# A hybrid decoder layer on one core: the first key chunk takes the place of the 112-column product, which moves into the fourth chunk, and x and the weights are loaded alternately

## The reference, cut to what matters

```python
u = rms_norm(h, norm_mix_w)
proj = u @ w_in                      # [256, 2048] @ [2048, 17504], float32
(q, k_c, v_c, k_s, v_s, k_w, v_w, nsa_gate, z, xbc, dt_raw, branch_gate) = split(proj)
o_nsa = nsa_mixer(q, k_c, ..., nsa_gate, cos, sin, compression weights)   # compressed, selected, window
o_ssm = mamba2_mixer(z, xbc, dt_raw, ...)
merged = sigmoid(gate_a) * (o_nsa @ w_proj_nsa) + sigmoid(gate_b) * (o_ssm @ w_proj_ssm)
h = h + merged @ w_out
h = h + square(relu(rms_norm(h, norm_mlp_w) @ w_up)) @ w_down
out = rms_norm(h, norm_final_w)
```

## Time and profile before

| quantity | value |
|---|---|
| runs | 2144.05, 2144.53, 2145.13 us (median 2144.53) |
| profiled execution, own time | 2145.07 us |
| its span, first to last instruction | 2143.3 us |
| TensorE busy | 98% of the span |
| VectorE, ScalarE, GpSimd busy | 61%, 46%, 9% |
| mean DMA rate over the span | 175 GB/s |
| mean granted TensorE clock | 0.997 |

### The profile page before, as it was taken

The page is one execution under the profiler, slowest core; times in us unless marked ns, Lnnn a source line. Parts: engine busy times, 40 slices in busy tenths (PEclk is TensorE's granted clock), DMA queues, the critical chain, the costliest instruction groups (busy, mean ns, idle before and its releaser), DMA issues.

```text
span 2143.3 us, 28254 instructions
## 1 busy us (share of the span) xinstructions
PE 2098.7 (98%) x9822; PEld 1742.4 (81%) x9822; DVE 1315.3 (61%) x1653; ACT 979.7 (46%) x1339; POOL 186.3 (9%) x226
## 2 busy tenths in 40 slices
PE   7999999999999999999999999999999999999997
PEld 5888888888888887778878778888888888888886
DVE  5646666666664677776577756555555555555554
ACT  5434545454543555554355544444434434444443
POOL 3000000000000033331133310000000000000000
PEclk9999999999999999999999999999999999999999
DMA  8556454545456655545645456556566566556653
GB/s 236 188 162 176 146 169 147 169 146 172 145 184 194 177 157 148 146 148 195 187 139 152 152 187 206 184 180 187 189 194 186 186 196 188 186 191 189 188 190 135
DMA packets 195448, 375.15 MB, mean 175 GB/s; under 512 B 16048, under 2 KB 16144, under 8 KB 194960
## 3 DMA queue, kind: packets, MB, share of 16 engines
q1 hardware_dynamic: 193152, 365.87, 55.9%
q0 software_dynamic: 2160, 7.79, 1.1%
q10 hardware_dynamic: 32, 0.01, 0.0%
HBM read 371.52 MB, written 2.10 MB: 174 GB/s over the span
## 4 chain that ended last, share of the span: by engine, by line
PE 52%; issue 41%; POOL 2%; DVE 1%; ACT 1%; DMA 1%; DVEq 1%; ACTq 0%; POOLq 0%; SPq 0%
PE acc L280 15%; PE acc L282 15%; PE acc L281 15%; PE x L813 1%; PE tr L303 1%; DMA raw<-w_in 1%; POOL ML L600 1%; POOL MH L600 1%; PE x L741 1%; PE x L696 1%; PE tr L763 1%; POOL XTOK L607 1%; PE x L803 0%; PE x L748 0%; PE tr L756 0%
## 5 line engine op out<-in xcount | busy, mean ns | idle before, releaser
L247 DVE TENSOR_TENSOR lo<-raw,hi 128x1024 fp32r<-128x1024 f32 (+1 forms) x696 | 861.3, 1246 | 617.1 <-ACT hi L240 606.6
L240 ACT ACTIVATE hi<-raw 128x1024 fp32r<-128x1024 f32 (+1 forms) x696 | 726.7, 1051 | 676.4 <-PE acc L282 650.6
L280 PE MATMUL acc<-hi,LAh 128*128 128x512 f32 x1856 | 737.5, 397 | 5.0 <-DVE lo L247 5.0
L282 PE MATMUL acc<-hi,LAl 128*128 128x512 f32 x1856 | 724.1, 390 | 0.0
L281 PE MATMUL acc<-lo,LAh 128*128 128x512 f32 x1856 | 723.2, 390 | 0.0
L280 PEld LDWEIGHTS acc<-hi,LAh 128*128 128x128 f32 x1856 | 348.6, 188 | 80.1 <-DVE lo L247 5.3
L282 PEld LDWEIGHTS acc<-hi,LAl 128*128 128x128 f32 x1856 | 348.4, 188 | 73.5
L281 PEld LDWEIGHTS acc<-lo,LAh 128*128 128x128 f32 x1856 | 348.7, 188 | 72.2 <-issue 1.7
L280 PE MATMUL acc<-hi,LBh 128*128 128x512 f32 x896 | 352.1, 393 | 3.2 <-DVE LBl L335 3.2
L282 PE MATMUL acc<-hi,LBl 128*128 128x512 f32 x896 | 349.8, 390 | 0.0
L281 PE MATMUL acc<-lo,LBh 128*128 128x512 f32 x896 | 349.7, 390 | 0.0
(11 more groups left out here) (271 smaller groups left out, 1258.5 us busy)
## 6 DMA issues: line engine op xcount, KB each, us to landing
raw<-w_in SPq DMA_DIRECT2D x304, 512.0 KB, 3.8
raw<-w_up SPq DMA_DIRECT2D x128, 512.0 KB, 3.8
raw<-w_down SPq DMA_DIRECT2D x128, 512.0 KB, 4.5
raw<-w_proj_ssm SPq DMA_DIRECT2D x64, 512.0 KB, 4.2
raw<-w_proj_nsa SPq DMA_DIRECT2D x32, 512.0 KB, 4.6
raw<-w_out SPq DMA_DIRECT2D x32, 512.0 KB, 4.5
GA<-x SPq DMA_DIRECT2D x4, 512.0 KB, 6.0
GA<-cmp_k_w POOLq DMA_DIRECT2D x4, 512.0 KB, 8.9
```

What stands on the lines that cost most here:

```text
L240: act.activation(hi[:, sl, :, 0:n], raw[:, sl, :, 0:n], ACT.Copy).then_inc(s_hi, 1)
L247: dve.tensor_tensor(lo[:, sl, :, 0:n], raw[:, sl, :, 0:n], hi[:, sl, :, 0:n].bitcast(F32), ALU.subtract).then_inc(s_lo, 1)
L280: pe.matmul(o, xh, wh, start=(k == 0), stop=False)
L282: x = pe.matmul(o, xl, wh, start=False, stop=(k == KT - 1))
```

## The change

- C_SMALL is dropped from the row of chunks; C_KC is number 0, all later numbers fall by one, and the two accumulator pairs are swapped for them.
- SP issues x quarter 0, groups 0 and 1 of C_KC, quarter 1, group 2, quarter 2, groups 3 and 4, quarter 3, groups 5 to 7. Group 4 waits for `s_lo` 1, and quarter 3 stands behind it.
- TensorE turns quarters 0 and 1, then multiplies group 0 and turns quarter 2 behind it, and turns quarter 3 behind group 3. Groups 0, 2, 4 and 6 wait for the low parts of quarters 0 to 3. ScalarE and VectorE split in the matching order.
- ScalarE does a one-element copy right after the constants are made, so that its first table load comes there.
- The sums of squares move to slots 3 and 4 of C_KC; the take of C_KC waits for the norm factors.
- The 112 columns: POOL loads all their weights (48 and 64 columns of 2048 rows) into GA after `compress(0)`; ScalarE and VectorE split them whole in C_VS into `LBh` and `LBl`; TensorE multiplies them in four parts behind groups 3 to 6 of C_VS into bank x7. The copy, turn, gates, softplus, cumulative sums and the rest of that chain move into C_VS slot 7, C_KW and C_VW.
- `columns`, `angles` and both `reduce_angles` move to slots 1, 3 and 4 of C_VC, `sines` to its slot 5. `compress_k2` no longer waits for the step sizes.
- The quarters of the compression weights wait for `s_lo` 4 to 18 in twos.

```diff
-C_SMALL, C_KC, C_VC, C_KS, C_VS, C_KW, C_VW, C_AT = 0, 1, 2, 3, 4, 5, 6, 7
+C_KC, C_VC, C_KS, C_VS, C_KW, C_VW, C_AT = 0, 1, 2, 3, 4, 5, 6
...
+            load_x(0)
+            load_group(sp, C_KC, 0, w_in, 0, KC0)
+            load_group(sp, C_KC, 1, w_in, 0, KC0)
+            load_x(1)
+            load_group(sp, C_KC, 2, w_in, 0, KC0)
+            load_x(2)
+            load_group(sp, C_KC, 3, w_in, 0, KC0)
+            load_group(sp, C_KC, 4, w_in, 0, KC0)
+            load_x(3)
+            for j in (5, 6, 7):
+                load_group(sp, C_KC, j, w_in, 0, KC0)
...
-                    pool.wait_ge(s_lo, 8 * n + 2 * q + 6)
+                    pool.wait_ge(s_lo, 8 * n + 2 * q + 4)
...
+            pool.wait_ge(s_hid, 1)
+            pool.dma_start(SMG, w_in[:, :, NG0:NG0 + 3 * NH]).then_inc(s_smw, 16)
+            pool.dma_start(SMD, w_in[:, :, DT0:DT0 + SH]).then_inc(s_smw, 16)
...
+            def small(q):
+                pe.wait_ge(s_sml, 2)
+                o = X7[0:SMALL, 0:S]
+                for k in range(4 * q, 4 * q + 4):
+                    wh, wl = LBh[:, k, 0:SMALL], LBl[:, k, 0:SMALL]
                     pe.matmul(o, wh, LAh[:, k, :], start=(k == 0), stop=False)
                     pe.matmul(o, wh, LAl[:, k, :], start=False, stop=False)
                     x = pe.matmul(o, wl, LAh[:, k, :], start=False, stop=(k == KT - 1))
...
             def compress_k2():
                 pe.wait_ge(s_hs, 1)
                 pe.wait_ge(s_w2, 32)
-                pe.wait_ge(s_dts, 3)
+                pe.wait_ge(s_colc, 2)
...
+            turn_x(0)
+            turn_x(1)
+            mm_chunk(pe, C_KC, 0, LAh, LAl, {0: [lambda: turn_x(2)], 3: [lambda: turn_x(3)]},
+                     need={0: [(s_trd, 1)], 2: [(s_trd, 2)], 4: [(s_trd, 3)], 6: [(s_trd, 4)]})
+            mm_chunk(pe, C_VC, 1, LAh, LAl, {0: [turn_columns], 2: [lambda: pe_turn(pe, E_KC, XR, [(s_acc, C_KC + 1)])],
                                              6: [lambda: compress(0)]})
...
+                                             3: [lambda: small(0)], 4: [lambda: small(1)], 5: [lambda: small(2)],
+                                             6: [lambda: small(3)]})
+            mm_chunk(pe, C_KW, 0, LAh, LAl, {0: [turn_small], 6: [cumsum]})
...
+            act.wait_ge(s_const, 1)
+            act.activation(SS2[:, 0, 0:1], mhalf[:, 0:1], ACT.Copy)
...
+            split_x(0)
+            split_hi(act, C_KC, 0)
+            split_x(1)
+            split_hi(act, C_KC, 1)
+            split_hi(act, C_KC, 2)
+            split_x(2)
...
+            slots(act, split_hi, C_KC, 8, {2: [lambda: split_x(3)], 3: [lambda: squares_of_x(0)], 4: [lambda: squares_of_x(1)],
+                                           7: [take_kc]})
+            slots(act, split_hi, C_VC, 8, {2: [lambda: copy_t(E_KC, KV[:, 0:2, :])], 5: [sines], 6: [lambda: hidden(0, 1)],
+                                           7: [lambda: take(C_VC, 1, XR[:, 0, :])]})
...
+            slots(act, split_hi, C_VS, 8, {0: [small_hi], 2: [lambda: copy_t(E_KS, key_cols(0, 0))],
+                                           7: [lambda: take(C_VS, 1, V_(0, 0)), copy_small]})
+            slots(act, split_hi, C_KW, 8, {1: [gates_dt], 2: [softplus], 7: [lambda: take(C_KW, 0, XR[:, 0, :])]})
...
+            slots(dve, split_lo, C_KC, 8, {2: [lambda: split_x(3)], 7: [take_kc]})
+            slots(dve, split_lo, C_VC, 8, {1: [columns], 2: [lambda: blocks(0, E_KC, CPK)], 3: [angles, lambda: reduce_angles(0)],
+                                           4: [lambda: reduce_angles(1)], 6: [lambda: hidden(0)],
+                                           7: [lambda: take(C_VC, 1, XR[:, 1, :], C_VC + 1)]})
...
+            slots(dve, split_lo, C_KW, 8, {1: [gates_dt], 3: [softplus], 6: [cumsums], 7: [lambda: take_rope(C_KW, 0, C_KW + 1)]})
```

More of the change, by code:

```diff
@@ L158, in build @@
         s_w2 = sem("compression_second_weights_landed")
+        s_smw = sem("small_weights_landed")
+        s_smh = sem("small_high_parts")
+        s_sml = sem("small_low_parts")
+        s_smm = sem("small_multiplied")
+        s_sma = sem("first_small_rows_taken")
+        s_smd = sem("second_small_rows_taken")
         s_smt = sem("gates_copied")
@@ L452, in _, with load_x @@
         def _(sp):
-            for n in range(4):
+            def load_x(n):
                 sp.dma_start(GA[:, :, NC * n:NC * (n + 1)], x_rows[:, :, NC * n:NC * (n + 1)]).then_inc(s_x[n], 16)
+            load_x(0)
[9 more added lines that the diff above has]
+                load_group(sp, C_KC, j, w_in, 0, KC0)
             w_na = a["w_proj_nsa"].rearrange("(k p) c -> p k c", p=P)
@@ L459, in _ @@
             w_dn = a["w_down"].rearrange("(k p) c -> p k c", p=P)
-            load_chunk(sp, C_SMALL, w_in, 0, 0, extra=[(w_in, NG0, 0, 3 * NH), (w_in, DT0, 3 * NH, SH)])
-            for C, c0 in ((C_KC, KC0), (C_VC, VC0), (C_KS, KS0), (C_VS, VS0), (C_KW, KW0), (C_VW, VW0)):
+            for C, c0 in ((C_VC, VC0), (C_KS, KS0), (C_VS, VS0), (C_KW, KW0), (C_VW, VW0)):
                 load_chunk(sp, C, w_in, 0, c0)
@@ L650, in _, with turn_x @@
             pe.transpose(X6[:, 0:16], NAT[0:16, 4, :], identf[0:16, 0:16]).then_inc(s_colp, 1)
-            for n in range(4):
+            def turn_x(n):
                 free = [(s_tra, 2 * n - 2), (s_trd, n - 1)] if n > 1 else []
                 pe_turn(pe, E_U + n, GA[:, :, NC * n:NC * (n + 1)], [(s_x[n], 16)] + free, banks=UB[n % 2], sm=s_tr)
[L656 to L662, removed]
+            def small(q):
[3 more added lines that the diff above has]
+                    wh, wl = LBh[:, k, 0:SMALL], LBl[:, k, 0:SMALL]
                     pe.matmul(o, wh, LAh[:, k, :], start=(k == 0), stop=False)
@@ L950, in hidden @@
                 act.activation(HT[:, :], X7[:, 0:NG * NCMP], ACT.Tanh, scale=0.5).then_inc(s_hta, 1)
[L952 to L955, removed]
@@ L956, in _, with take_kc @@
-            slots(act, split_hi, C_KS, 8, {2: [lambda: copy_t(E_VC, KV[:, 0:2, :])], 6: [lambda: hidden(1, 4)],
[L957 to L962, removed]
+            def take_kc():
+                act.wait_ge(s_rx, 1)
+                take(C_KC, 0, XR[:, 0, :])
@@ L1152, in _, with split_x @@
             dve.drain().then_inc(s_colc, 1)
-            for n in range(4):
+            def split_x(n):
                 dve_split_t(dve, E_U + n, LAh, LAl, 4 * n, COLS[:, CN1 + 4 * n:CN1 + 4 * n + 4], banks=UB[n % 2])
-                if n == 1:
-                    for j in range(LEAD):
-                        split_lo(dve, C_SMALL, j)
+            split_x(0)
+            split_lo(dve, C_KC, 0)
+            split_x(1)
+            split_lo(dve, C_KC, 1)
+            split_lo(dve, C_KC, 2)
+            split_x(2)
             def columns():
@@ L1288, in take_rope, with small_lo @@
                 rope()
[L1290 to L1294, removed]
+            def small_lo():
+                for n, (c0, c1, src) in enumerate(((0, 3 * NH, SMG), (3 * NH, SMALL, SMD))):
+                    dve.wait_ge(s_smh, n + 1)
+                    dve.tensor_tensor(LBl[:, :, c0:c1], src, LBh[:, :, c0:c1].bitcast(F32), ALU.subtract).then_inc(s_sml, 1)
@@ L1295, in _ @@
             dve.wait_ge(s_sin, 4)
             slots(dve, split_lo, C_KS, 8, {1: [key_rope], 2: [lambda: blocks(1, E_VC, CPV)], 5: [key_copy],
[L1297 to L1300, removed]
@@ L1301, in _ @@
-            slots(dve, split_lo, C_VW, 8, {2: [lambda: copy_t(E_KW, key_cols(1, 2))],
-                                           7: [lambda: take(C_VW, 0, V_(1, 1), C_VW + 1)]})
+                                           6: [lambda: hidden(1)], 7: [lambda: take_rope(C_KS, 0, C_KS + 1)]})
+            slots(dve, split_lo, C_VS, 8, {1: [value_copy, small_lo], 2: [lambda: copy_t(E_KS, key_cols(0, 2))],
+                                           7: [lambda: take(C_VS, 1, V_(1, 0), C_VS + 1)]})
+            slots(dve, split_lo, C_KW, 8, {1: [gates_dt], 3: [softplus], 6: [cumsums], 7: [lambda: take_rope(C_KW, 0, C_KW + 1)]})
@@ L1304, in maxima @@
+            slots(dve, split_lo, C_VW, 8, {1: [low_steps], 2: [lambda: copy_t(E_KW, key_cols(1, 2))],
+                                           7: [lambda: take(C_VW, 1, V_(1, 1), C_VW + 1)]})
             def maxima(n):
```

76 lines of the change are left out of this document (39 added, 37 removed).

## The result

Four runs of the changed kernel took 2130.53 to 2132.57 us, median **2131.86**; four of the kernel before, on the same chip, had a median of 2144.44 (2144.05 to 2145.13). The ratio is 0.9941, with a 95% interval of 0.9928 to 0.9953: 12.6 us faster (10.1 to 15.4 us by the interval). The profiled execution took 2130.53 us, the shortest of the four; its span is 2128.8. The forecast was 2135.5, between 2132 and 2141.

What follows compares the result with a forecast made beforehand. TensorE's 16.65 us without work before 58.3 us, plus a low clock at the start, were taken as the bound. Idle time 6.0, restarts 2.2 and clock 0.8 sum to 9.0 us: from 2144.53 to 2135.5, range 2132 to 2141.

Steps and rivals of the forecast that it cites:

- Idle time: TensorE's idle time before 58.3 us falls from 16.65 to 10.6 us: 6.0 us saved.
- The second quarter: At the start, x's quarter 1 becomes the fourth 512 KB load: new TensorE wait of 3.35 us, ends 1.7 and 5.0.
- Points 3 and 5: TensorE's waits around the small product (4.2 and 1.5 us) and in C_KC (5.0 and 1.2 us) go.
- Rival B: VectorE falls behind again with the angles in C_VC; hardly more than 1.4 us won, 2143; chance 0.08.
- The table load: ScalarE's first table load moves under the wait for x; worth nothing, the first low part is early enough anyway.
- `cmp_k_w1`: First compression weights, issued at 37 us, land near 52, before `compress(0)` near 58: hidden by 5 us or so.
- Rival E: Slower: `cmp_k_w1` arrives late at `compress(0)`; 2150 if it landed at 73 us; chance 0.05.
- Point 7: At `compress_k2`, TensorE newly waits 2.5 us for the second compression weights (26.1 against 23.6); ends 0 and 4.7.
- rival A: Second compression weights come in time at `compress_k2`; 2.5 + 0.3 us more won, 2132.7; chance 0.15.
- Restarts: In the start, eight fewer TensorE restarts after waits, 0.28 us each: 2.2 us saved.
- Clock: In the start, two turns fewer at 1.2 GHz, but 0.95 us lost in group 0: 0.8 us saved.
- rival C: Clock rises later, since only products count: 3.66 us after 12.1 or near 18; 1 to 2.5 us lost, 2137.5; chance 0.10.

Runs made afterwards that it cites:

- e5: Changed kernel with x's quarter 1 loaded ahead of group 1 and quarter 2 ahead of group 2; 2129.38 us.
- e9: Kernel before with only the angles, both reductions and the sines moved from C_KC to C_VC; 2143.22 us, ratio 0.9992.
- e10: Changed kernel without ScalarE's one-element copy, so its first table load stands before its first split again; 2132.36 us.
- e2: Changed kernel with the second compression weights behind one more wait, for s_lo 20; 2136.17 us.
- e1: Kernel before with five more, long satisfied waits on GpSimd; 2142.57 us, ratio 0.9991.
- e12: Changed kernel with only TensorE's pause near 1253 us filled by 20 dummy transposes; 2130.86 us.
- e6: Changed kernel with the second compression weights loaded ahead of all first ones; 2132.61 us.
- e7: Changed kernel with 20 dummy transposes ahead of the turns of quarters 0 and 1, and the second compression weights loaded first; 2130.94 us.
- e8: Changed kernel with early dummy transposes, second weights first, quarters 1 and 2 loaded earlier, and 20 dummy transposes in the pause near 1253 us; 2128.82 us.
- e4: Changed kernel with 8 and 12 dummy transposes on TensorE ahead of the turns of quarters 0 and 1; 2129.56 us.
- e11: e8 with five more satisfied waits on GpSimd; 2127.62 us, ratio 0.9920 against the kernel before.

## Why the prediction came out so

Of the 3.6 us that the forecast missed, 1.5 lie in its own sum (9.0 against a lead of 10.5 us) and 2.1 in code that it put at nothing. The sum, point by point, against the lead of 10.5 us in the one pair of profiles:

1. Idle time. Forecast 6.0 us saved, measured 16.65 - 8.1 = 8.5. The constants as forecast; x's first quarter 0.4 us later (1.74 instead of 1.34).
2. The second quarter: 2.6 us of new wait, forecast 3.35. Right in kind, 0.7 us too high. e5 confirms that its place in the queue sets it.
3. Points 3 and 5, the waits for VectorE: all gone, none new. Rival B did not happen. In e9 the waits of C_KC's groups fall to 0.7 us with the angles gone, against 5.0 and 3.1 in the two profiles that have them there.
4. The table load: put at nothing, 0.27 us in e10. The reason given, that the low part is there before TensorE has turned quarter 1, does not hold: it came 0.27 us late there.
5. `cmp_k_w1`: no wait. Rival E did not happen.
6. **Point 7, the second compression weights, is the step that failed.** The chain of ten terms in front of them was right: forecast 17.7 us behind the keys' turn. The landing was mis-sized. The prediction took the longer of two loads seen before, 6.7 us; it was 4.5. As a forecast wait this made 2.5 us of what was 0.4. The view of line 577 in the changed kernel:

```profile
L577 POOL DMA_DIRECT2D BCT<-cmp_k_w x1: 563/563/563, 65.9 to 65.9; - x1
L577 POOL DMA_DIRECT2D BCT<-cmp_v_w x1: 542/542/542, 66.5 to 66.5; - x1
...
DMA to landing us min/median/max: 4.5/4.5/4.5
```

66.5 + 4.5 = 71.0, and TensorE was there at 70.7. That was rival A, given 0.15. e2 shows that the wait itself is real and paid in full when it is made. Why the landing was shorter is open. During the 6.7 us SP's queue moved 1.6 MB and during the 4.5 us 0.9 MB, with 0.7 MB of GpSimd's own queue in both; so what was queued beside it is the likely reading. But the later of the two loads took 5.4 us in e1 and 7.8 in e9, in nearly the kernel before, and 4.3 to 5.6 in changed kernels with the same order of loads by GpSimd: no single value would have been safe.
7. Restarts: forecast 2.2. What is left of the lead, 10.5 - 8.5 + 0.1 = 2.1, is as large. It is a remainder and was not measured by itself; with the lead of 11.0 at 225 us it would be 2.6.
8. Clock: forecast 0.8 us saved, 0.1 us lost in this profile. Two turns ran at the low clock as forecast, but nine matmuls of group 0 did (1.9 us) where 0.95 us was forecast. The lag of 3.66 us was measured once and varies: the clock rose at 15.8 us here, but at 13.4 and 13.5 in e10 and e12, at 14.5 in e2 and 14.8 in e6, with TensorE going on at 9.9 to 10.2 each time. With three slow matmuls (e10, e12) the term would have been some 1.1 us saved, so the size of this miss is that of one execution.

8.5 + 2.1 - 0.1 = 10.5. With 2.1 us for the weights put right, the forecast would have been 11.1 for this part, and 2133.4 for the time.

The range had a slip of its own. Its lower end, 2132, was to be rival A with an earlier second quarter; that is 2132.7 - 1.65, about 2131, below the measured 2131.86. And its upper end takes 1.6 us for the clock where the text gives 1.8.

**What was missing altogether** is the part near 1253 us. The prediction treated all code behind the seventh chunk as unchanged, and it is; from that it put the effect there at nothing. Yet GpSimd's slow step went away (0.94 us: the lead grows from 10.52 to 11.46), the following pause was 0.6 us shorter, and in the profiled execution the fall of the clock was gone (2.5 us). In the medians the fall counts for less than in this pair, since it comes and goes: 10.5 + 0.9 leaves about 1 us of the 12.6. That this is the share of the falls is an estimate and smaller than the interval of the measured gain: the start alone differs by over 1 us between profiles (leads of 11.0 and 12.2), and no run fills the pause in the kernel before. In the changed kernel filling it brought 1.0 us. The mechanism of the slow step is shown in part: five profiles have it (before, e6, e7, e8, e9), each with one transfer of the instruction queue that starts in the last 0.3 us or less of the step, and the nine others have neither, at 0.72 to 0.73 us. That GpSimd waited for those instructions is not shown, and the times speak against this transfer as the cause: it starts 1.35 to 1.71 us into a step of 1.66 to 1.79 us and takes 0.31, so that in four of the five it ends after the step. Both may follow from the same place in the stream; the cause stays open.

In the profiled execution the clock rose where rival C had put it, 3.66 us after 12.1, but not for its reason. The Trainium skill (TensorE: Matmul & The Clock Gate, Part 4) has transposes not counted as activity; e4 says otherwise, with turn 1 at 1.09 us behind transposes alone. And in the other profiles with this start the clock rose up to 2.5 us earlier.

## What to carry to other kernels

Where other traffic may delay a load, take the landing times of several profiles as the two ends (3.2 to 7.8 us here for the same 64 KB) and give the wait between them no single likeliest value.

A change moves instructions in code that it does not touch. Look for pauses there: five satisfied waits in an engine's stream took 1 us off a step over 1000 us later, and moving two loads put it back on.

A pause of TensorE of some 3 us among products cost the pause and, in seven of eleven profiles, 3.4 or 6.8 us at half the clock on top. Transposes of a constant into a free PSUM bank took that away in all three profiles that had them, and ahead of the first real work they also brought the high clock earlier (e4). And compare more than one profile of each kernel before a term of 1 us is put down to a cause: the clock alone moved the start by that much.

## What the runs showed of the hardware that was not expected

- A `pow` of GpSimd over 128x2 elements took 1.66 to 1.79 us instead of 0.72 to 0.75, always together with an 8 KB transfer of the instruction queue in the same 3 us. Five satisfied waits a thousand microseconds earlier in its stream turned it off (e1, e11); moving two loads turned it on (e6).
- TensorE's clock rises on transposes alone: in e4 the 12 dummies from 7.30 us on take 1.65 us, where 8 took 1.97 at 3.83 us, before any product of a group.
- The same start reached the high clock at 13.4 to 15.8 us, from one execution to the next.
- The clock fell in thin stretches as well as in pauses: in e1 and e9 from about 21 us on, in the waits of the 112-column product, which the changed kernel no longer has.
- A small load by GpSimd, 64 KB, took 3.2 (e2) to 7.8 us (e9) to land; the traffic beside it differed.
